# SBUF offsets modulo 256 bytes in a gated DeltaNet and SwiGLU block: the large buffers move down by 64 bytes, the token sums stay

## What is computed

```python
proj = rms_norm(h, norm_mix_w) @ w_in            # q, k, v, z, two logits, p, two gates
o    = gated_delta_rule_chunked(l2(q), l2(k), v, beta, g)
y_a  = (rms(o) * o_norm_w * silu(z)) @ w_proj_a
y_b  = pool(p) @ w_proj_b
h    = h + (sigmoid(gate_a) * y_a + sigmoid(gate_b) * y_b) @ w_out
h    = h + (silu(hn @ w_gate) * (hn @ w_up)) @ w_down     # 2048 -> 5632 -> 2048
out  = rms_norm(h, norm_final_w)[:, 16:]
```

## The kernel before, in words

| stage | moving | stationary |
|---|---|---|
| projections | 192, 0, 64, 128 in turn with k (halves: also 32 further) | 128 |
| merge | 192 | 128 |
| output | ring of three: 192, 128, 192 | `out_act` 128, 192, 192, 128, 128, 192, 192 (A11, A12, S2, S1, S3, S4, A22) |
| gate and up | 192 | `hi_a`, `lo_a`, `hi_b`, `hi_c` 128; `lo_b`, `lo_c`, `hi_2`, `lo_2` 192 |
| down | ring of three: hi 128 lo 128; hi 128 lo 192; hi 192 lo 192 | 192 |

## Time and profile before

### The profile page before, as it was taken

How to read it: one execution, slowest core, us unless ns; L and a number is a source line. 1 busy time by engine, 2 the same in 40 slices (tenths; PEclk the granted TensorE clock), 3 DMA queues, 4 the chain that set the end, 5 groups by cost and what they waited for, 6 DMA issues and landing times.

```text
span 2764.5 us, 44509 instructions
## 1 busy us (share of the span) xinstructions
PE 2694.2 (97%) x17640; PEld 2449.9 (89%) x17640; DVE 1836.5 (66%) x1771; ACT 998.2 (36%) x1025; POOL 339.0 (12%) x350
## 2 busy tenths in 40 slices
PE   8999999999999999998989999999999998999997
PEld 7999988888889977887879999999999997788885
DVE  4444555555553234557888788878888887888886
ACT  4443322222222232223344444444444443333333
POOL 5000044444442410100000000000000000000000
PEclk9999999999999999999999999999999999999998
DMA  4333222222223334678333544454445449756661
GB/s 142 92 91 91 77 77 77 77 82 76 83 76 92 106 91 154 226 268 306 131 126 125 173 146 148 144 174 144 148 144 174 144 137 317 232 187 204 220 206 61
DMA packets 345651, 398.69 MB, mean 144 GB/s; under 512 B 11481, under 2 KB 300386, under 8 KB 344418
## 3 DMA queue, kind: packets, MB, share of 16 engines
q1 hardware_dynamic: 286514, 334.34, 37.5%
q10 hardware_dynamic: 59072, 63.44, 6.7%
HBM read 325.92 MB, written 71.83 MB: 144 GB/s over the span
## 4 chain that ended last, share of the span: by engine, by line
PE 92%; DVE 3%; issue 2%; DMA 1%; ACT 1%; POOL 0%; SPq 0%; DVEq 0%; ACTq 0%; POOLq 0%
PE psum L1946 34%; PE psum L2258 10%; PE psum L2257 10%; PE psum L2256 10%; PE psum L2233 6%; PE psum L2234 6%; PE psum L2235 6%; PE psum L2106 2%; PE psum L2101 1%; PE psum L1896 1%; PE psum L1924 1%; DMA w_raw<-in_w_proj_a 1%; PE psum L2085 1%; DVE hq L1606 1%; PE psum L2178 0%
## 5 line engine op out<-in xcount | busy, mean ns | idle before, releaser
L1946 PE MATMUL psum<-hn_lo,w_hi 128*128 128x264 f32 (+1 forms) x1600 | 453.5, 332 | 0.0
L1946 PE MATMUL psum<-hn_hi,w_lo 128*128 128x264 f32 (+1 forms) x1600 | 453.2, 332 | 0.0
L1946 PE MATMUL psum<-hn_hi,w_hi 128*128 128x264 f32 (+1 forms) x1600 | 452.6, 332 | 0.0
L1272 DVE TENSOR_TENSOR w_lo<-w_raw,w_hi 128x1024 fp32r<-128x1024 f32 x176 | 227.0, 1291 | 335.6 <-ACT w_hi L870 335.0
L870 ACT ACTIVATE w_hi<-w_raw 128x1024 fp32r<-128x1024 f32 x176 | 185.0, 1056 | 455.5 <-PE psum L1946 381.5
L1946 PEld LDWEIGHTS psum<-hn_hi,w_hi 128*128 128x128 f32 x1600 | 270.4, 189 | 23.0 <-issue 0.2
L1946 PEld LDWEIGHTS psum<-hn_lo,w_hi 128*128 128x128 f32 x1600 | 269.4, 188 | 23.9 <-issue 0.7
L1946 PEld LDWEIGHTS psum<-hn_hi,w_lo 128*128 128x128 f32 x1600 | 269.8, 189 | 23.0
L2233 PE MATMUL psum<-dn_hi,act_hl 128*128 128x512 f32 x616 | 244.5, 397 | 14.1 <-DVE hq L1606 13.0
L2234 PE MATMUL psum<-dn_lo,act_hl 128*128 128x512 f32 x616 | 244.0, 396 | 0.0
L2235 PE MATMUL psum<-dn_hi,act_hl 128*128 128x512 f32 x616 | 243.0, 394 | 0.0
(11 more groups left out here) (350 smaller groups left out, 6254.6 us busy)
## 6 DMA issues: line engine op xcount, KB each, us to landing
w_raw<-in_w_in SPq DMA_DIRECT2D x144, 512.0 KB, 3.6
ffn_raw<-in_w_ffn_gate SPq DMA_DIRECT2D x44, 1024.0 KB, 6.5
ffn_raw<-in_w_ffn_up SPq DMA_DIRECT2D x44, 1024.0 KB, 6.5
dn_raw<-in_w_ffn_down SPq DMA_DIRECT2D x40, 1024.0 KB, 7.1
act_hl<-act_dram SPq DMA_DIRECT2D x70, 512.0 KB, 9.0
act_dram<-comb_hi ACTq DMA_DIRECT2D x22, 896.0 KB, 4.2
act_dram<-comb_lo ACTq DMA_DIRECT2D x22, 896.0 KB, 6.2
out_raw<-in_w_out SPq DMA_DIRECT2D x16, 1024.0 KB, 10.3
```

Of the source, the lines that this page charges most:

```text
L1272: dve.tensor_tensor(wlo[s][:], raw[s][:], whi[s][:].bitcast(F32), ALU.subtract).then_inc(S["lo_ready"], 1)
L1946: ins = pe.matmul(o, lhs, r, start=kt == 0 and i == 0, stop=kt == 4 * n_chunks - 1 and i == 2)
```

## The change

`small` gives up 16 unused columns (144 for 160; two of its slices move from columns 130 and 138 to 128 and 136), `vec_b` is put right behind it, and both share 768 bytes for the 832 of before. Everything behind them moves down by 64 bytes and so starts at 128 modulo 256, as the weight buffers do. `s_at`, from which the gate and up tokens and all that is placed behind them (`after_s`: `ffn_raw1`, `comb`, `sg`, two of the `dn_raw`) are counted, becomes `hn_at + 64`: these keep their old addresses, with the tokens at 192 modulo 256. The down stage's `act_hl`, `t3_buf`, `hq` and third ring pair are now counted from `hn_at`, so they move to 128 too. The assertions only check the offsets.

```diff
+BEAT = 256
...
-        small = place("small", [P, 160])
-        vec_b = place("vec_b", [P, 2 * KT + HEADS + 1])
+        small_at = top[0]
+        small = place("small", [P, 144])
+        vec_b = place("vec_b", [P, 2 * KT + HEADS + 1], at=small_at + 144 * 4)
+        top[0] = small_at + 768
+
         mixer_consts_at = top[0]
+        assert whi_at % BEAT == wlo_at % BEAT == mixer_consts_at % BEAT
...
+        assert hn_at % BEAT == whi_at % BEAT
...
+        assert ext_at % BEAT == whi_at % BEAT
...
-        s_at = hn_at
+        s_at = hn_at + 64
...
-        act_hl = [place(f"act_hl{i}", [P, 2, 4, UNIT], F32R, at=s_at + i * 8192) for i in range(7)]
-        t3_buf = place("t3_buf", [P, 4, BLOCK], at=s_at + 7 * 8192)
-        hq = place("hq", [P, 4, 2, 2, BLOCK], at=s_at + 4 * 16384)
-        ring_at = [(whi_at, whi_at + 8192), (wlo_at, ext_at), (s_at + 6 * 16384, s_at + 6 * 16384 + 8192)]
+        act_hl = [place(f"act_hl{i}", [P, 2, 4, UNIT], F32R, at=hn_at + i * 8192) for i in range(7)]
+        t3_buf = place("t3_buf", [P, 4, BLOCK], at=hn_at + 7 * 8192)
+        hq = place("hq", [P, 4, 2, 2, BLOCK], at=hn_at + 4 * 16384)
+        ring_at = [(whi_at, whi_at + 8192), (wlo_at, ext_at), (hn_at + 6 * 16384, hn_at + 6 * 16384 + 8192)]
...
-        gcur, bcur = (small[:, 0:8], small[:, 130:138]), (small[:, 8:16], small[:, 138:146])
+        gcur, bcur = (small[:, 0:8], small[:, 128:136]), (small[:, 8:16], small[:, 136:144])
```

## The result

The changed kernel took 2761.43 us, the median of 14 executions, beside 2767.39 for the kernel before in the same session (2764.53 to 2769.12): a ratio of 0.995, 95% interval 0.993 to 0.9969. That is 6 us for the 37.9 that the sum gave. The median hides the finding. The 14 times lie in two groups with nothing between them: four at 2729.5 to 2733.0 us, around the predicted 2730.2, and ten at 2759.2 to 2765.8. The kernel before has one group, here and in every later session (103 executions in all, 2764.2 to 2770.4 us). A kernel on one core, with the same data and the same instructions, has two durations 31 us apart.

The account below looks back on a forecast made before the run. The prediction took the rate of successive TensorE matmuls, set by operand offsets modulo 256 bytes, as the bound. Savings of 25.6, 8.6, 2.0 and 1.7 us summed to 37.9, giving a median of 2730.2 us, range 2722 to 2746.

Parts of the forecast that it names:

- the four terms: Forecast savings by stage: gate and up 25.6 us, down 8.6, output 2.0, merge 1.7.
- merge: Merge stage: 768 matmuls go from 229.0 to 226.7 ns, saving 1.7 us.
- Output: Output stage: 15 of 28 products that don't pair equal offsets gain, saving 2.0 us.
- Down: Down stage after its first two units: 1680 matmuls go from 231.8 to 226.7 ns, saving 8.6 us.
- two early units: Down's first two units: set by loads and VectorE, so 0, with 1 us each way allowed for transfers.
- The projections: Projections on hn: the moving tile's offsets only rotate, so 0, within 4 us.
- the first term: Gate and up: every product at 113.3 ns a matmul, units of 19.04 us for 19.63, saving 25.6 us.
- Rival 1: Whole kernel: offsets aren't the cause of the rates, so nothing changes, 2768.1 us; chance 0.03.
- Rival 2: Gate and up: 256 bytes isn't the period, only S2 reaches 113.3 ns, 2748.8 us; chance 0.07.
- Rival 3: Down and output: something else holds them, so their 10.6 us are missing, 2740.8 us; chance 0.04.
- Rival 4: Merge, output and down: equal offsets are bad for 512 columns too, 28.9 us lost, 2771.4 us; chance 0.03.
- a loss unseen: Whole kernel: the rest of the chances, a loss the prediction didn't see, no size given; chance 0.01.

Follow-up runs that it names:

- e7: Changed kernel with PE made to wait before A22 in every gate-and-up unit until VectorE has finished all of c; 2892.1 and 2892.9 us.
- e15: Changed kernel with S2's weights back at 192, equal to the tokens, plus a PE wait before A22 in each unit; 2897.14 us, one execution.
- e13: Changed kernel with S2's two weight tiles (and t2) back at 192, equal to the tokens; 2740.49 us, ratio 0.9903 to the kernel before.
- e5: Changed kernel with lo_c alone 64 bytes further, at 192, so S4 and A22 are mixed; 2741.77 us, ratio 0.9917 to the kernel before.
- e6: Changed kernel with hi_2 alone 64 bytes further, at 192, so only S2 is mixed; 2737.82 us, ratio 0.992 to the kernel before.
- e2: Changed kernel with the gate and up tokens at 128, equal to all weights; 2779.23 us, ratio 1.0041 to the kernel before.
- e3: Changed kernel with down's act_hl, t3_buf, hq and third ring pair back at 192; 2771.6 us, ratio 1.0011 to the kernel before.
- e4: Changed kernel with the gate and up tokens at 0, 128 bytes further than the weights; 2769.54 us, ratio 1.0006 to the kernel before.
- e14: Repeat of the changed kernel with S2's weights at 192, equal to the tokens; 2739.88 us, ratio 0.9893 to the kernel before.
- e10: Changed kernel with the tokens at 64 and PE made to wait before A22 in each unit; 2889.8 and 2893.3 us.

## Why the prediction was wrong

**Where the short step holds, the four terms stand.** In the profiled execution of the lower group gate and up saved 25.4 us (stage spans 887.1 and 861.7) for 25.6 forecast, and merge 1.1 for 1.7. Output saved 1.4 for 2.0 by its span. Its products from the fourth to the 26th alone saved 1.8; the rest is how long PE waits in the second and third, which makes the span 171.1 to 173.7 us over the 16 traces with this output stage. Down saved 6.3 us for 8.6: 8.2 in the ten later units, of which the first took 38.47 us and the others 38.08, and its two early units took 1.9 us more (56.9 for 55.0), where I had put 0 with 1 us for the transfers. In the 15 traces with this down stage they took 54.3 to 57.0 us, so one profile can't say that the change costs these 1.9. The profiled execution came to 2732.96 us for 2728.8. The projections moved by 0.5 us, inside their 4.

**The step that failed** is the first term's: "every product is paired as A11 and A12 are: a unit becomes 168 x 113.3 = 19.04 us". It took the rate for a function of the pair of offsets. The runs show that moving 192 over stationary 128 has two rates at 256 columns, 113.3 and 117.8 ns, each of which keeps itself up as long as the same kind of product follows. PE's last restart, 1.6 us of waiting before A22 of the first unit, picks one for the remaining 43 units. At this offset it picked the long one in 31 executions of 37 by their times, and so did 43 restarts of 43 in e7 and 40 of 43 in e15. In the upper group's traces the unit is 19.79 us, longer than the 19.63 of the earlier trace rows, and gate and up loses 43 x 0.16 = 7 us where it should gain 25; what is left of the sum is what down, output and merge bring.

**What the kernel before had shown.** Its A11 and A12 ran at 113.3 ns in the earlier trace rows, in a unit with an S2 of equal offsets and four mixed products. e13 and e15 show what an equal product does: it draws the chain to the short step and never from it. That mixed products do some of the same follows from e5 and e6. The change removed both, S2's equal pair to save 0.16 us and the mixed ones to save 0.43; which of them did it in the kernel before no run separates. And its trace held the warning, which the prediction read past, since it took one unit for all. These are the starts of A11 and S2 in the second unit, the first one behind the wait of the earlier trace rows:

```profile
1454.62 0.28 PE L2256 MATMUL psum<-s_hi,hi_a 128*128 128x256 f32 x1
...
1460.27 0.28 PE L2256 MATMUL psum<-s_hi,hi 128*128 128x256 f32 x1
```

A11 and A12 take 5.65 us, 117.7 ns each, and in all 42 units behind it 5.44 us: the same tiles, the same offsets, the long step once. A second hint stands in the rows: the merge and the fifteenth output product are both moving 192 over stationary 128, and ran at 229.0 ns and 232.9. One pair of offsets with two rates says that something besides the pair decides.

**The rivals.** Rival 1 (the offset isn't the cause) is out by e2, e3 and e4, which move tiles alone. Rival 2 is out: S1 to A22 run at A11's rate in both groups, whatever their distance above 256. Rival 3 is out, as down's units are 38.08 us in both groups. Rival 4 is out, as merge and down with all operands equal stay at 226.7 ns (21.76 us for 96, 38.08 for 168). The true rival, a rate that depends on what ran before, was not among them, and the chances left it the 0.01 for a loss unseen. Six executions of 37 lie inside the range that was given; the other 31 are above its end.

**What stays open.** No run shows what in TensorE or its memory makes the two steps, nor why a restart leads mostly to the long one with the tokens at 192 and to the short one at 64. What decides a single restart is open too: its timing against VectorE, ScalarE and the loads was not varied by itself. The shares with a wait in each unit are of one profiled execution each. Whether tokens at 64 together with an equal product would be short in every execution wasn't tried. Of the versions run, S2 equal (e13, e14) gives the surest gain, 2740 us in eight of eight; tokens at 64 the lowest median, 2732 to 2733, at the price of the upper group in 3 of 20.

## What to carry to other kernels

A rate read from a few products in a mixed sequence is a rate of that sequence: before a stage is made uniform, look for the same pair of operands at two rates elsewhere in the trace. Where matmuls follow one another without a gap for thousands, time a change in many executions and look at all the times, since one restart may decide the stage and one profile shows one draw. A slightly worse product now and then can be worth keeping, if it is what draws the chain back: here 0.16 us in each unit bought back 0.75.

## What the runs showed of the hardware

With the weights at 128 modulo 256 bytes, a 128x256 matmul at the 2.4 GHz level started every 120 ns with the moving operand at the same offset (e2), every 118.7 with it 128 further (e4), and every 113.3 or 117.8 with it 64 or 192 further, the same instructions in the same order. At 512 columns equal offsets were the best seen, at 226.7 ns. The choice between 113.3 and 117.8 fell at restarts of PE. With a wait in each unit the restart led to the short step 0 times of 43 (e7) and 3 of 43 (e15) at 64 further, and 35 of 43 at 192 further (e10). Whole executions were short in 6 of 37 and 17 of 20. A step once taken held for up to 7,250 matmuls; an equal product in between changed the long to the short one in 31 of 40 passages. That one core, alone, with nothing in its program changed, can give times 31 us apart for this reason was not expected; the state is in the pace of the engine, not in its clock (0.99 granted over gate and up in both) and not in its waits.
